# A two-layer encoder on one core: attention masks as extra contraction rows, and high and low tokens in one matmul

## The chip, the cores and the metric

The kernel runs on one core of one Trainium2 chip. The metric is the device time of one execution in microseconds (us). The kernel before takes 827.09 us, the median of three runs from 827.08 to 827.15 us.

## What is computed

Two equal layers over 256 tokens of width 1024, float32. One layer, cut to what matters:

```python
u = rms_norm(x, g_mix_pre)
qa, ka, va, cq, ckv, ga, gb = split(u @ w_in)
# A: 16 query heads, 2 key/value heads of 64; query chunk c (64 tokens) reads key chunks c-1 and c; a sink per head
y_a = swa_sink_attention(rope(qa), rope(ka), va, sinks)
# B: 8 heads of 96 (64 + 32 rotary) from low-rank projections; query chunk c reads key chunks 0..c
y_b = mla_attention(qb, kb, vb)
mixed = sigmoid(ga + b0) * (y_a @ w_oa) + sigmoid(gb + b1) * (y_b @ w_ob)
x = x + rms_norm(mixed @ w_out, g_mix_post)
h = square(relu(rms_norm(x, g_mlp_pre) @ w_mlp_in)) @ w_mlp_out        # 1024 -> 4096 -> 1024
x = x + rms_norm(h, g_mlp_post)
```

Scores that a chunk must not see are set to -1e30 before the softmax.

## The kernel before

Every big product is made of three matmuls on rounded operands: high token times high weight, high token times low weight, low token times high weight. ScalarE copies each weight piece that arrives (`raw`) into a rounded high part (`w_hi`, L582), VectorE subtracts it for the low part (`w_lo`, L853). A piece is at most 128 x 1024 numbers; four high and four low pieces form a ring, so ScalarE may write piece p only when TensorE has used piece p-4 (`piece_used`). Loads are issued by SyncE in order of the pieces.

The order on each engine is written out by hand. One layer goes through:

1. Input projections (pieces 0 to 19), low-rank projections (20 to 27). Between them the rotary turns: VectorE turns the queries of token tile 0, GpSimd everything else (`pool_rope`). TensorE transposes the turned keys (`kA`) and queries (`qA`), VectorE copies the transposes out of the PSUM banks `tp0`, `tp1` (`turned_copy`, L901 to L909).
2. Attention: 18 groups of heads (`QUANTA`): four of kind A on token tile 0 (four heads x 128 keys each), eight of kind A on tile 1 (two heads x 192 keys), two of kind B on tile 0 (four heads x 128 keys), four of kind B on tile 1 (two heads x 256 keys). Step i of 20 on TensorE is: scores of group i, transposes of the probabilities of group i-2, one weight piece of the gate or output products, values of group i-2, and what `EXTRA` lists (a transpose of some q, k or y). The scores (L1251) are float32 matmuls, each recorded as two, with 64 rows of contraction in kind A and 96 in kind B. Behind the heads of a group stands one matmul (L1252) that adds the mask: `chunk_of` (which chunk a query is in) times `mask` (-1e30 or 0 for each key), 256 columns for both kinds of A and B on tile 0, 128 for B on tile 1. Both operands are written once by GpSimd at the start.
3. Output products, the first residual and norm.
4. The MLP, in eight blocks of 512 hidden features. In blocks 1 to 7 the input product (`mlp_in`, L1415 to L1417) has the weights as stationary operand and 256 tokens as moving one: for each of 4 pieces, 4 groups of 128 features and 2 rows of tiles it issues high x high, low tokens x high weights, high tokens x low weights, all into the banks `sc0` and `sc1`. Block 0 goes another way (`first_product`). ScalarE takes the ReLU out of the banks (L650), GpSimd squares it (L493), ScalarE and VectorE split it again (L658, L893), and the output product (`mlp_out`) of a block runs one block later. Blocks 2 to 6 are a loop on every engine.

## Time and profile before

| | |
|---|---|
| median of the runs | 827.09 us |
| profiled execution, its own time | 826.92 us |
| its span in the trace | 825.0 us |
| TensorE matmul busy | 803.2 us (97%), 4613 instructions |
| TensorE weight load busy | 696.4 us (84%) |
| VectorE busy | 509.8 us (62%) |
| ScalarE busy | 408.0 us (49%) |
| GpSimd busy | 125.2 us (15%) |
| chain that ended last | TensorE 92%, VectorE 4%, ScalarE 3% |

The chain that ended last is the row of instructions that sets the end, followed back from the last one. Recorded matmuls overlap: each has a length of its own (a 256-column one 283 ns), while the next starts earlier. What one costs is therefore read from start to start.

### The profile page before, as it was taken

The numbers are of one execution on the slowest core, as the hardware profiler recorded it, in microseconds if no ns is written. First come the engines' busy times: TensorE is split into PE (matmuls) and PEld (weight loads), VectorE is DVE, ScalarE is ACT, GpSimd is POOL, SyncE is SP. The second block draws the span as 40 slices with busy tenths as digits, with TensorE's granted clock in tenths as the row PEclk, the third lists the DMA queues.
The fourth block names the chain that finished last, engine by engine and source line by source line (L and its number), as shares of the span: only waits on it lengthen the run. The fifth ranks groups of instructions, "written<-read, shape, count | busy, mean of one in ns | idle before, by whom it ended". The sixth has DMA issues, their size and how long they took to land.

```text
span 825.0 us, 12057 instructions
## 1 busy us (share of the span) xinstructions
PE 803.2 (97%) x4613; PEld 696.4 (84%) x4613; DVE 509.8 (62%) x685; ACT 408.0 (49%) x747; POOL 125.2 (15%) x204
## 2 busy tenths in 40 slices
PE   6999999999999999999989999999999999999997
PEld 5987878888779999999879788788878899999995
DVE  5768766575785555545566877566576844555554
ACT  5757434444474444444466574444346654444452
POOL 2443000001231000000114420000031200000000
PEclk9999999999999999999999999999999999999999
DMA  7647422334636555565327482331436565565521
GB/s 236 234 159 265 166 71 85 102 102 153 203 115 224 180 186 170 196 203 191 97 72 267 160 297 80 102 102 54 151 126 209 176 201 171 189 200 173 186 103 51
DMA packets 68462, 132.21 MB, mean 160 GB/s; under 512 B 2842, under 2 KB 10564, under 8 KB 68164
## 3 DMA queue, kind: packets, MB, share of 16 engines
q1 hardware_dynamic: 68276, 131.12, 47.9%
q8 instruction: 27, 0.44, 0.2%
q10 hardware_dynamic: 144, 0.52, 0.2%
q14 instruction: 15, 0.12, 0.1%
HBM read 130.59 MB, written 1.05 MB: 160 GB/s over the span
## 4 chain that ended last, share of the span: by engine, by line
PE 92%; DVE 4%; ACT 3%; issue 0%; DMA 0%; POOLq 0%; ACTq 0%; POOL 0%; DVEq 0%
PE acc L1167 17%; PE acc L1169 17%; PE acc L1168 17%; PE sc L1417 7%; PE sc L1416 7%; PE sc L1415 7%; PE tp L1144 5%; PE acc L1283 5%; PE sc L1251 4%; PE acc L1201 4%; ACT s_hi L605 2%; DVE w_lo L853 1%; ACT w_hi L582 1%; PE sc L1167 1%; PE sc L1169 1%; PE sc L1168 1%
## 5 line engine op out<-in xcount | busy, mean ns | idle before, releaser
L853 DVE TENSOR_TENSOR w_lo<-raw,w_hi 128x1024 fp32r<-128x1024 f32 (+3 forms) x256 | 312.8, 1237 | 187.9 <-ACT w_hi L582 186.3
L582 ACT CAST w_hi<-raw 128x1024 fp32r<-128x1024 f32 (+3 forms) x256 | 252.3, 995 | 217.8 <-PE acc L1169 146.6
L1167 PE MATMUL acc<-w_hi,s_hi 128*128 128x512 f32 (+3 forms) x680 | 263.0, 387 | 3.7 <-DVE w_lo L853 3.7
L1168 PE MATMUL acc<-w_lo,s_hi 128*128 128x512 f32 (+3 forms) x680 | 257.6, 379 | 0.0
L1169 PE MATMUL acc<-w_hi,s_lo 128*128 128x512 f32 (+3 forms) x680 | 257.6, 379 | 0.0
L1167 PEld LDWEIGHTS acc<-w_hi,s_hi 128*128 128x128 f32 x680 | 127.9, 188 | 27.9 <-DVE w_lo L853 5.6
L1169 PEld LDWEIGHTS acc<-w_hi,s_lo 128*128 128x128 f32 x680 | 127.8, 188 | 24.0
L1168 PEld LDWEIGHTS acc<-w_lo,s_hi 128*128 128x128 f32 x680 | 128.0, 188 | 21.1
L1415 PE MATMUL sc<-s_hi,w_hi 128*128 128x256 f32 x448 | 126.9, 283 | 0.0
L1417 PE MATMUL sc<-s_hi,w_lo 128*128 128x256 f32 x448 | 126.8, 283 | 0.0
L1416 PE MATMUL sc<-s_lo,w_hi 128*128 128x256 f32 x448 | 126.8, 283 | 0.0
L1415 PEld LDWEIGHTS sc<-s_hi,w_hi 128*128 128x128 f32 x448 | 85.9, 192 | 0.8 <-DVE w_lo L853 0.3
L1416 PEld LDWEIGHTS sc<-s_lo,w_hi 128*128 128x128 f32 x448 | 85.9, 192 | 0.5
L1417 PEld LDWEIGHTS sc<-s_hi,w_lo 128*128 128x128 f32 x448 | 85.9, 192 | 0.0
L493 POOL TENSOR_TENSOR tok<-k_b 128x512 f32<-128x512 f32 x32 | 36.5, 1160 | 266.1 <-ACT k_b L650 266.1
L669 ACT ACTIVATE probs<-sc,neg_m 128x128 f32<-128x128 f32 (+2 forms) x96 | 37.7, 403 | 46.5 <-DVE neg_m L945 32.9
L537 POOL TENSOR_TENSOR tok<-gate_a,gate_b 128x512 f32<-128x512 f32 x8 | 14.1, 1783 | 260.6 <-DVE gate_b L993 260.6
L602 ACT ACTIVATE s_hi<-tp 128x512 fp32r<-128x512 f32 x24 | 13.7, 596 | 48.7 <-PE tp L1144 48.7
L942 DVE TENSOR_REDUCE row_max<-sc 128x2 f32<-128x384 f32 (+2 forms) x36 | 22.6, 627 | 13.8 <-PE sc L1252 13.8
L605 ACT ACTIVATE s_hi<-tp,gain 128x128 fp32r<-128x128 f32 x76 | 21.2, 382 | 15.3 <-PE tp L1144 15.3
L650 ACT ACTIVATE k_b<-sc 128x512 f32<-128x512 f32 x28 | 15.2, 595 | 25.4 <-PE sc L1417 25.4
L883 DVE SCALAR_TENSOR_TENSOR s_lo<-tp,gain,s_hi 128x128 fp32r<-128x128 f32 x76 | 20.7, 343 | 8.8 <-ACT s_hi L605 8.6
(143 smaller groups left out, 779.0 us busy)
## 6 DMA issues: line engine op xcount, KB each, us to landing
raw<-in_w_mlp_in SPq DMA_DIRECT2D x32, 1024.0 KB, 5.3
raw<-in_w_mlp_out SPq DMA_DIRECT2D x32, 1024.0 KB, 5.0
raw<-in_w_in SPq DMA_DIRECT2D x24, 1024.0 KB, 5.4
raw<-in_w_oa SPq DMA_DIRECT2D x8, 1024.0 KB, 5.0
raw<-in_w_out SPq DMA_DIRECT2D x8, 1024.0 KB, 5.0
raw<-in_w_ob SPq DMA_DIRECT2D x4, 1024.0 KB, 5.1
raw<-in_w_in SPq DMA_DIRECT2D x4, 768.0 KB, 4.6
raw<-in_w_in SPq DMA_DIRECT2D x4, 576.0 KB, 7.0
```

The lines of the kernel that those rows point to most:

```text
L582: s.copy(split_view(w_hi, p), raw_view(p)).then_inc(hi_ready, 1)
L605: ins = s.activation(dst[:, k, :], src[:, k, :], ACT.Copy, scale=gain[:, col + k:col + k + 1])
L669: ins = s.activation(probs[:, i % 2, a * w + skip:(a + 1) * w], sc[i % 2][:, a * w + skip:(a + 1) * w], ACT.Exp, bias=neg_m[:, c + a:c + a ...
L853: v.tensor_tensor(split_view(w_lo, p), raw_view(p), split_view(w_hi, p).bitcast(F32), ALU.subtract)\
L1144: ins = nc.tensor.transpose(b[0:rows, i * P:(i + 1) * P], src, ident[:, :])
L1167: mm(banks[t][:, 0:N], h[:, kk, tk], wh[:, k, :], start=(start and k == 0), stop=False)
L1168: mm(banks[t][:, 0:N], h[:, kk, tk], wl[:, k, :], start=False, stop=False)
L1169: ins = mm(banks[t][:, 0:N], low[:, kk, tk], wh[:, k, :], start=False, stop=(stop and k == b - a - 1))
L1283: ins = mm(y[:, (h + a) * 64:(h + a + 1) * 64], pt, vv, start=(b == 0), stop=(b == w // P - 1))
L1415: mm(out, wh[:, k, cols], s1_hi[:, kk, :], start=(i == 0 and k == 0 and f % 2 == 0), stop=False)
L1416: mm(out, wh[:, k, cols], s1_lo[:, kk, :], start=False, stop=False)
L1417: ins = mm(out, wl[:, k, cols], s1_hi[:, kk, :], start=False, stop=(i == 3 and k == 1 and f % 2 == 1))
```

## The change

Three things change.

- Masks. The transposed queries and keys get extra rows in the contraction: two for kind A (64 becomes 66), four for kind B (96 becomes 100). In the query's tile row c is 1 for the queries of chunk c, in the key's tile row c is -1e30 for keys that chunk c must not see. The mask matmul, `chunk_of` and `mask` go. GpSimd writes the rows once, in layer 0, behind the first norm (`chunk_rows`, 20 instructions). For this the queries of kind A stand one head in one tile column, all with partitions 0 to 63, and the tile holds one token tile at a time; the keys of its two heads stand beside each other. The copies out of the transposes become four for the keys (was one) and two for each query transpose (was one). The order of `EXTRA` changes.
- Input product of the MLP, blocks 2 to 7. High and low tokens stand in one tile (`s1_both`); one matmul of 512 columns does high x high and low x high, one of 256 columns does high tokens x low weights. The two halves of a bank hold two partial sums, so the product uses four banks (`sc0`, `sc1`, `tp0`, `tp1`).
- VectorE adds the two halves (`sum_h`, four reductions a block) into `k_b`, and ScalarE takes the ReLU there.

```diff
+            consts = Steps(pool, consts_ready)
+            def chunk_rows(view, low, high, inside, outside):
+                rows, heads, n = view.shape
+                head = view[:, 0, :]
+                consts.link(g.memset(head, inside))
+                consts.link(g.affine_select(out=head, in_=head, compare_op=ALU.is_ge, fill=outside,
+                                            base=-CHUNK * low, pattern=[[1, n]], channel_multiplier=-CHUNK))
...
+                consts.link(g.tensor_copy(view[:, 1:, :], head.unsqueeze(1).to_broadcast([rows, heads - 1, n])))
...
+                if l == 0:
+                    pool.wait_ge(rstd_ready, TT)
+                    chunk_rows(qT_a[AD:AK, :, :], 0, 0, 1.0, 0.0)
+                    chunk_rows(kT_a[AD:AK, :, A_AT[0]], -1, 0, 0.0, NEG)
+                    chunk_rows(kT_a[AD:AK, :, A_AT[1]], 0, 1, 0.0, NEG)
+                    chunk_rows(qT_b[BQK:BK, :, :], 0, 0, 1.0, 0.0)
+                    chunk_rows(kT_b[BQK:BK, :, :], 1 - NCHUNK, 0, 0.0, NEG)
...
+            def relu_of_sum(pos, j):
+                for b in range(2):
+                    act.wait_ge(h_summed, pos.count(TT * (MJ - 2), TT * (j - 2) + b + 1, TT))
+                    s.activation(k_b[:, b, 0:COL], k_b[:, b, 0:COL], ACT.Relu).then_inc(relu_done, 1)
...
+            def sum_h(pos, j, p):
+                dve.wait_ge(piece_used, pos.count(NP, RING + p + 1, 8))
+                for b in range(2):
+                    dve.wait_ge(h_ready, pos.count(TT * MJ, TT * (j - 1) + b + 1, TT))
+                    for f in range(2):
+                        bank = h_banks[2 * b + f]
+                        ins = v.tensor_reduce(k_b[:, b, f * SEQ:(f + 1) * SEQ],
+                                              bank[:, :].rearrange("p (a n) -> p n a", a=2), AX, ALU.add)
+                    ins.then_inc(h_summed, 1)
...
-                    ins = v.tensor_copy(kT_a[:, :], b[:, 0:SEQ])
+                    for g in range(AKV):
+                        for t in range(TT):
+                            ins = v.tensor_copy(kT_a[0:AD, g, A_AT[t]], b[g * AD:(g + 1) * AD, A_KEYS[t]])
...
+                    for odd in range(2):
+                        ins = v.tensor_copy(qT_a[0:AD, g * AG + odd:(g + 1) * AG:2, :],
+                                            b[odd * AD:(odd + 1) * AD, :].rearrange("p (h n) -> p h n", h=AG // 2))
...
-                    mm(b[:, a * w + skip:(a + 1) * w], q, k, start=(a == 0), stop=False)
-                mm(view, chunk_of[r0:r1, :], mk, start=False, stop=True).then_inc(scores_ready, 1)
+                    ins = mm(b[:, a * w + skip:(a + 1) * w], q, k, start=(a == 0), stop=(a == n - 1))
+                ins.then_inc(scores_ready, 1)
...
+                            for k in range(2):
+                                kk = 2 * i + k
+                                mm(bank[:, :].rearrange("p (a n) -> p a n", a=2), wh[:, k, cols], s1_both[:, :, kk, :],
+                                   start=(i == 0 and k == 0), stop=False)
+                                ins = mm(bank[:, SEQ:2 * SEQ], wl[:, k, cols], s1_hi[:, kk, :], start=False,
+                                         stop=(i == 3 and k == 1))
```

TensorE, step 4 of the attention (first group of kind A on tile 1), before. `tp`, `sc` and `acc` are PSUM banks, `probs` the probabilities of the group two steps back:

```order
L1283 MATMUL acc<-kv_a,probsT 128x64 x4
L1144 MATMUL tp<-ident,k_b 96x128 x4
L1251 MATMUL sc<-kT_a,qT_a 128x192 x2
L1252 MATMUL sc<-mask,chunk_of 128x4x64
L1144 MATMUL tp<-ident,probs 128x128 x4
L1167 MATMUL acc<-w_hi,s_hi 128x512
```

The same place on TensorE in the changed kernel:

```order
L1312 MATMUL acc<-kv_a,probsT 128x64 x4
L1181 MATMUL tp<-ident,tok 128x128 x4
L1280 MATMUL sc<-kT_a,qT_a 128x192 x2
L1181 MATMUL tp<-ident,probs 128x128 x4
L1204 MATMUL acc<-w_hi,s_both 128x512
```

The mask matmul is gone, and the transpose ahead of the scores is now one of queries (`tok`), since `EXTRA` is in another order.

VectorE, between the low-rank projections and the first scores, before. The weight pieces behind the copies are those that the last low-rank product and the first gate product need:

```order
L853 TENSOR_TENSOR w_lo<-raw,w_hi 128x512 x2
L901 COPY kT_a<-tp 128x256
L904 COPY qT_a<-tp 128x4x128 x2
L1062 TENSOR_SCALAR neg_sink<-sink_in 128x16
L853 TENSOR_TENSOR w_lo<-raw,w_hi 128x512 x2
L853 TENSOR_TENSOR w_lo<-raw,w_hi 128x1024 x3
```

The same place on VectorE in the changed kernel:

```order
L873 TENSOR_TENSOR w_lo<-raw,w_hi 128x512 x2
L933 COPY kT_a<-tp 64x128
L933 COPY kT_a<-tp 64x192
L933 COPY kT_a<-tp 64x128
L933 COPY kT_a<-tp 64x192
L937 COPY qT_a<-tp 64x4x128 x4
L1095 TENSOR_SCALAR neg_sink<-sink_in 128x16
L873 TENSOR_TENSOR w_lo<-raw,w_hi 128x512 x2
```

Three copies have become eight, in front of the same weight pieces.

VectorE in the MLP loop, from the split of a finished block to the weight pieces of the output product, changed kernel:

```order
L913 TENSOR_TENSOR s_lo<-tok,s_hi 128x512
L872 REGISTER_ALU
L873 TENSOR_TENSOR w_lo<-raw,w_hi 128x1024
L872 REGISTER_ALU
L873 TENSOR_TENSOR w_lo<-raw,w_hi 128x1024
L917 REGISTER_ALU
L919 REGISTER_ALU
L922 TENSOR_REDUCE k_b<-sc 128x256 x2
L919 REGISTER_ALU
L922 TENSOR_REDUCE k_b<-tp 128x256 x2
L873 TENSOR_TENSOR w_lo<-raw,w_hi 128x1024
```

In the kernel before, the two reductions and their register instructions aren't there; the weight pieces follow each other.

## Rows read from the trace of the kernel before

**Rows 1.** Windows: length; busy us (count) of PE, PEld, DVE, ACT, POOL; clock.
```profile
73.00:160.00 87.00, 87.00 (x496) 71.38 (x496) 56.59 (x104) 41.36 (x118) 0.15 (x1) 1.00 0.36 117
262.00:400.00 138.00, 138.00 (x882) 126.02 (x881) 71.75 (x63) 65.30 (x76) 12.25 (x12) 1.00 0.57 186
```
**Rows 2.** Waits of TensorE: total us, times, longest.
```profile
PE acc L1167 <- DVE w_lo L853: 3.7, 4, 1.4
```
**Rows 3.** Timeline of TensorE in the MLP: start, length, instruction.
```profile
299.77 0.28 PE L1415 MATMUL sc<-s_hi,w_hi 128*128 128x256 f32 x1
...
301.09 0.28 PE L1417 MATMUL sc<-s_hi,w_lo 128*128 128x256 f32 x1
...
301.91 0.40 PE L1167 MATMUL acc<-w_hi,s_hi 128*128 128x512 f32 x1
...
311.89 0.39 PE L1169 MATMUL acc<-w_hi,s_lo 128*128 128x512 f32 x1
```
**Rows 4.** Groups by form, TensorE: busy us, mean ns.
```profile
L1415 PE MATMUL sc<-s_hi,w_hi 128*128 128x256 f32 x448 | 126.9, 283 | 0.0
```
**Rows 5.** Timeline of TensorE, step 2 of the attention (kind A).
```profile
80.93 0.60 PE L1144 MATMUL tp<-ident,tok 128*128 128x128 f32 x4
81.46 1.16 PE L1251 MATMUL sc<-kT_a,qT_a 64*128 64x128 f32 x8
82.37 0.36 PE L1252 MATMUL sc<-mask,chunk_of 64*128 64x256 f32 x1
82.67 0.66 PE L1144 MATMUL tp<-ident,probs 128*128 128x128 f32 x4
83.08 0.48 PE L1167 MATMUL acc<-w_hi,s_hi 128*128 128x512 f32 x1
```
**Rows 6.** Timeline of TensorE, step 13 of the attention (kind B).
```profile
147.56 0.61 PE L1144 MATMUL tp<-ident,tok 128*128 128x128 f32 x4
148.00 1.06 PE L1251 MATMUL sc<-kT_b,qT_b 96*128 96x128 f32 x8
148.81 0.36 PE L1252 MATMUL sc<-mask,chunk_of 128*128 128x256 f32 x1
149.02 0.60 PE L1144 MATMUL tp<-ident,probs 128*128 128x128 f32 x4
149.37 0.48 PE L1167 MATMUL acc<-w_hi,s_hi 128*128 128x512 f32 x1
```
**Rows 7.** Timeline of VectorE ahead of the first scores.
```profile
66.19 0.42 DVE L901 COPY kT_a<-tp 128x256 f32<-128x256 f32 x1 [0.43 <-PE tp L1144]
66.62 1.43 DVE L904 COPY qT_a<-tp 128x512 f32<-128x512 f32 x2
...
68.22 0.68 DVE L853 TENSOR_TENSOR w_lo<-raw,w_hi 128x512 fp32r<-128x512 f32 x1
```
**Rows 8.** Timeline of TensorE: first matmul of weight piece 26.
```profile
69.92 0.39 PE L1167 MATMUL acc<-w_hi,s_hi 128*128 128x512 f32 x1
```
**Rows 9.** Groups by form, VectorE.
```profile
L917 DVE COPY probsT<-tp 64x256 f32<-64x256 f32 x16 | 6.6, 415 | 0.0
L942 DVE TENSOR_REDUCE row_max<-sc 128x2 f32<-128x512 f32 x8 | 5.5, 688 | 9.6 <-PE sc L1252 9.6
```
**Rows 10.** Timeline behind the input product of one MLP block.
```profile
368.67 1.09 ACT L650 ACTIVATE k_b<-sc 128x512 f32<-128x512 f32 x2 [1.83 <-PE sc L1417]
...
370.73 3.00 DVE L853 TENSOR_TENSOR w_lo<-raw,w_hi 128x1024 fp32r<-128x1024 f32 x2 [2.63 <-ACT w_hi L582]
...
376.66 0.39 PE L1167 MATMUL acc<-w_hi,s_hi 128*128 128x512 f32 x1
```
**Rows 11.** GpSimd: its costliest group, and the stretch behind the first norm.
```profile
L493 POOL TENSOR_TENSOR tok<-k_b 128x512 f32<-128x512 f32 x32 | 36.5, 1160 | 266.1 <-ACT k_b L650 266.1
...
22.10:59.40 37.30, 37.30 (x216) 33.29 (x215) 26.11 (x37) 22.16 (x44) 16.00 (x23) 1.00 0.56 193
```
**Rows 12.** Timeline of TensorE at the start of layer 1.
```profile
418.94 1.48 PE L1201 MATMUL acc<-w_hi,s_hi 128*128 128x384 f32 x4
```

More of the change, by code:

```diff
@@ L86 @@
 NQ = len(QUANTA)
+CONST_STEPS = 20
 NSTEP = NQ + 2
@@ L206, in build @@
         ident = sb("ident", [P, P])
-        chunk_of = sb("chunk_of", [P, P], F32R)
-        mask = sb("mask", [P, 3, 2 * P], F32R)
         pos_i = sb("pos_i", [P, TT], I32)
@@ L447, in _ @@
             steps.link(ins)
-            sel, mk = chunk_of[:, :].bitcast(F32), mask[:, :, :].bitcast(F32)
-            steps.link(g.memset(sel, 0.0))
-            steps.link(g.memset(mk, 0.0))
-            for half in range(2):
-                r = 2 * 32 * half
-                steps.link(g.memset(sel[r:r + 1, 0:CHUNK], 1.0))
-                steps.link(g.memset(sel[r + 32:r + 33, CHUNK:P], 1.0))
-                steps.link(g.memset(mk[r:r + 1, 0, CHUNK:P], NEG))
-                steps.link(g.memset(mk[r:r + 1, 1:3, P + CHUNK:2 * P], NEG))
-                g.memset(mk[r + 32:r + 33, 1, CHUNK:P], NEG).then_inc(consts_ready, 1)
-                pool.wait_ge(consts_ready, half + 1)
             pool.wait_ge(sines, 2)
@@ L1234, in scores @@
                     pe.wait_ge(probs_ready, pos.count(NQ, i - 1))
-                r0, r1 = (64 * g, 64 * g + 64) if kind == "A" else (0, P)
-                which = 0 if t == 0 else (1 if kind == "A" else 2)
                 b = sc[i % 2]
-                k0 = w // P - 1 if kind == "B" else 0
-                nk = w // P - k0
-                view = b[:, :].rearrange("p (h k c) -> p h k c", h=n, c=P)[:, :, k0:, CHUNK:P]
-                mk = mask[r0:r1, which, 0:w].rearrange("p (k c) -> p k c", c=P)[:, k0:, CHUNK:P]\
-                    .unsqueeze(1).to_broadcast([r1 - r0, n, nk, CHUNK])
                 for a in range(n):
                     if kind == "A":
-                        q = qT_a[r0:r1, h + a, t * P:(t + 1) * P]
-                        k = kT_a[r0:r1, skip:w]
+                        q = qT_a[:, g * AG + h + a, :]
+                        k = kT_a[:, g, A_AT[t]]
                     else:
@@ L1288, in extra @@
                     _, t, h = name
-                    blocks = [tok[:, t, (4 * h + a) * AKV * AD:(4 * h + a + 1) * AKV * AD] for a in range(4)]
+                    blocks = [tok[:, t, (4 * h + a) * 2 * AD:(4 * h + a + 1) * 2 * AD] for a in range(4)]
                 elif name[0] in ("qB", "kB"):
@@ L1342, in _ @@
                 turned(pos, ("qA", 0, 1))
-                pe.wait_ge(consts_ready, 2)
+                pe.wait_ge(consts_ready, CONST_STEPS)
                 for i in range(NSTEP):
@@ L1418, in mlp_in, with mlp_in_wide @@
                         ins.then_inc(piece_used, 1)
+                def mlp_in_wide(pos, p):
+                    for i in range(4):
+                        pe.wait_ge(lo_ready, pos.count(NP, 2 * RAW + p + i + 1, 8))
+                        wh, wl = (split_view(w, p + i).rearrange("p (k n) -> p k n", k=2) for w in (w_hi, w_lo))
+                        for f in range(4):
+                            bank, cols = h_banks[f], slice(f * P, (f + 1) * P)
+                            for k in range(2):
[4 more added lines that the diff above has]
+                                         stop=(i == 3 and k == 1))
+                        ins.then_inc(piece_used, 1)
                 def h_is_split(pos, j):
```

45 lines of the change are left out of this document (28 added, 17 removed), and 4 rows, old and new, of the table EXTRA.

## The prediction, made before the changed kernel ran

> **What bounds the kernel now.** I read the page's busy shares first, then the windows by stage, then the waits of TensorE, and last its timeline from start to start. TensorE is busy in 87.00 of 87.00 us of the attention and in 138.00 of 138.00 us of the MLP, at full clock [rows 1]; VectorE, the next, is busy in 56.59 and 71.75 us of them. The only wait of TensorE on VectorE anywhere is 3.7 us in four pieces [rows 2], and none lies in those two stretches. So the reader should see a kernel whose length is the sum of TensorE's starts: a matmul less is time less, and work on another engine is free until its slack is used up. The question for each part is then what a removed or merged matmul costs from start to start, and whether the added work on VectorE, ScalarE or GpSimd comes late anywhere. The sums are made against the profiled execution, 826.92 us, which is 0.17 us below the median of the runs.
>
> **Input product of the MLP.** In a steady stretch twelve 256-column matmuls stand between 299.77 and 301.09, so 1.32 / 11 = 0.120 us each. Of the 512-column ones 45 stand between 301.91 and 311.89, so 9.98 / 44 = 0.2268 us each [rows 3]. Twice 0.120 is 0.240: one matmul of 512 columns is 0.0132 us cheaper than two of 256. The columns stay, one fixed part per matmul goes. L1415 runs 448 times, which is two layers by seven blocks by 32 [rows 4]; six of the seven blocks change, so 384 pairs are merged: 384 x 0.0132 = 5.1 us, all on TensorE's row of starts. The bounds: nothing, if the moving operand in two stretches or the two half banks cost what the merge saves; and 5.1 us. I take 5.1, since the 512-column row is the same operation with the same number of output columns.
>
> The Trainium skill speaks against this size: "TensorE: Matmul & The Clock Gate", section "Back-to-back issue gap", gives N / 2.4 + 2.5 ns for a warm matmul, which is 109 and 216 ns. By it a merge saves 2.5 ns, the 384 of them 1.0 us, and the total below would be 816.5 us. The trace shows 120 and 226.8 ns, a fixed part of 13 ns; the measurement decides.
>
> What it adds. VectorE does four reductions a block. The nearest row reduces 128x512 in 0.688 us [rows 9], so 2.75 us a block. Behind the input product ScalarE starts its ReLU at 368.67, VectorE ends the low part of the next weight piece half way through its pair of 3.00 us, at 370.73 + 1.50 = 372.23, and TensorE starts on that piece at 376.66 [rows 10]: 4.4 us of slack. In the changed kernel the piece waits in ScalarE's queue behind the ReLU, and the ReLU behind the sums: 368.67 + 2.75 + 0.55 (half of 1.09, the last ReLU) + 1.05 (the copy of a 1024-wide piece) + 1.50 = 374.5. That leaves 2.1 us. So the sums cost nothing: the cover is the first three pieces of the output product. Squares and second split shift by the same 2.3 us, and their user comes a block later.
>
> **Masks.** I compare a step of kind A with one of kind B, in which all else has the same sizes [rows 5, 6]. Kind A has 64 rows in the contraction, kind B 96. From the first transpose ahead of the scores to the first matmul of the product behind them it is 83.08 - 80.93 = 2.15 us in A and 149.37 - 147.56 = 1.81 us in B. The 0.34 us lie at the crossings: 0.09 more before the first score, 0.10 more within the eight records of the scores, 0.09 more behind the mask, 0.06 more in the transposes after it. With 66 rows I expect A to run as B does with 96, since the next row in size above 64 shows no such cost. The mask itself: in B the eight records and the mask take 149.02 - 148.00 = 1.02 us, and eight records at the pace of the transposes (0.44 / 4 = 0.11) take 0.88, so 0.14; a 256-column matmul in a steady row costs 0.12 [rows 3]. I take 0.12, and half of it for the 128-column masks.
>
> Per layer: 12 groups of kind A by (0.34 + 0.12) = 5.5 us, two of B on tile 0 by 0.12 = 0.24, four on tile 1 by 0.06 = 0.24; together 6.0, and 12.0 us for two layers. Bounds: 3.9 us (crossings stay, masks go) and 12.7 (0.14 for each mask). More rows in a float32 matmul add nothing that a row shows: 64 and 96 rows have the same columns and the same pace between.
>
> Here the skill bears the crossings out. "TensorEngine Tiling (Array Packing)", section "Key Properties", says that a change of tiling mode, and not of tile alone, drains TensorE, and its list of modes has 64 rows and 128 rows. By that rule 66 rows leave no change of mode and the saving is the 12.0 us; without it, with masks gone alone, it would be 3.9 us. The difference of the two steps above agrees with the rule.
>
> **Copies that get longer.** The key transposes are copied by four instructions of 64 partitions instead of one. A 64x256 copy takes 0.415 us [rows 9] and a 128x512 one 1.43 / 2 = 0.72 us, so a column costs 0.0012 us and the fixed part is about 0.11. Two of 128 and two of 192 columns: 1.2 us against 0.42 [rows 7], 0.8 more (bounds 0.4 and 1.24, four times the 64x256 row). The second query transpose on TensorE needs the bank that this copy frees, so 0.8 us come straight onto TensorE. The two query copies become four of the same length, as partitions don't shorten a copy (415 ns for 64): 1.43 us more. So VectorE reaches weight piece 26 at 68.22 + 2.2 = 70.4 and ends it at 71.1 us, while TensorE, itself 0.8 later, wants it at 69.92 + 0.8 = 70.7 [rows 7, 8]. Another 0.4 us of wait. Together 1.2 per layer, 2.4 us for two (bounds 0.8 and 4). Before, this wait did not exist, piece 26 was ready 1.0 us early; it is the one new wait that I expect. The next pieces and the row maxima start later by the same 2.2 us, but the steps of the attention give VectorE 30 us of idle time in 87 [rows 1]. The two later query copies (0.72 us more each, in steps 2 and 4) lie in it too.
>
> **GpSimd.** The 20 instructions on the rows handle 960 columns three times and copy 5824: 8704 columns. GpSimd's multiply of 512 takes 1.16 us [rows 11], 2.3 ns per column, so some 20 us; for two or four partitions I know no row, and bound it by 5 and 30. Between the first norm and the second query turn GpSimd is busy 16.00 of 37.30 us [rows 11], so 21.3 are idle. Behind the rows wait the two latent norms, the turn of the keys, the shared rotary key and one query turn; their first user on TensorE is the transpose of the keys at the end of this stretch. I take nothing, 0 to 1 us with what VectorE's own instructions lose beside it. TensorE's wait for `consts_ready` comes later still. The mask rows that GpSimd wrote at the start end nothing that was waited for.
>
> **The sum.** 826.92 - 5.1 - 12.0 + 2.4 = 812.2 us; on the median 812.4.
>
> **Rivals.**
> - A, the merge gives nothing: a two-stretch operand or two partial sums per bank slow the 512-column matmul by 13 ns. For it: no row has such an operand. Against: the mask's own operand was strided and kept its pace. Time: 812.4 + 5.1 = 817.5 us.
> - B, the change does not do what it says for the crossings: 66 rows cross as 64 do. Against: 96 rows don't. Time: 2 x 12 x 0.34 = 8.2 less saved, 820.6 us.
> - C, slower than before: the sums on VectorE. They read a bank with a stride of 256 columns, for which I have no row. If one takes r instead of 0.69 us, the weight piece behind is late once 4 (r - 0.69) exceeds 2.1, at r = 1.2. To lose all of the gain and 0.2% more, 16.4 us over 12 blocks, 1.4 us a block, r must be 1.56. At that point the time is 828.8 us or more. Against: the row maxima run at one column per 1.3 ns, and a stride inside a partition has to cost more than that again.
> - The clock: at the start of layer 1 matmuls of 384 columns start about 1.3 / 4 = 0.32 us apart (each ends 0.2 behind the next start, so 1.48 less 0.2 for four) [rows 12], where 384 columns at the pace of rows 3 take 0.12 + 128 x 0.00042 = 0.17: the clock is at its lower level, 1.2 GHz, behind the pause between the layers. In the changed kernel this stretch may fall away (1.6 us less, from some eleven such matmuls at 0.15) or come at another place. That is no case of its own, it widens the range.
>
> **How the numbers follow.** My forecast has 0.79; its own range is 809.5 to 815.5 (clock 1.6, copies from 0.8 to 4, GpSimd 1). A has 0.10, B 0.07, C 0.04. The range of 8 in 10 takes in A: 809.2 to 817.9. A measurement of this kernel tells a change from none at about 0.2%, 1.7 us: faster by more 0.94 (forecast, A and B, less 0.02), within 0.02 (A and B together with the worst of the copies), slower 0.04 (C).
>
> **What would show it.** Right: L1252 gone; in kind A the transposes, scores and transposes again as close as in kind B, 0.11 us apart; L1459 followed by its partner after 0.227 us and the pair 0.347 us long; TensorE busy all through the MLP; a wait of TensorE of 0.3 to 0.5 us on a `w_lo` ahead of the first scores and a gap of 0.8 in the query transposes, in both layers. Wrong: a wait on `w_lo` or `relu_done` in the MLP (C), a first score 0.1 us late (B), a 512-column matmul in 0.240 us (A), or GpSimd's rows reaching past 59 us with TensorE waiting on the keys.

## The result, and the profile after

The changed kernel takes 816.42 us (median of 4 runs, 815.82 to 818.57), the kernel before beside it 827.12 us: ratio 0.9881, 95% interval 0.9869 to 0.9894. That is 10.7 us faster. The forecast was 812.4 us, its range 809.2 to 817.9. The time lies in the range, 4.0 us above the forecast, and outside the 809.5 to 815.5 that the forecast had for itself. The profiled execution of the changed kernel took 818.57 us (span 816.6), the slowest of its four; part of the reason is the clock, shown below.

I compare the two profiled executions at the ends of the same weight pieces on TensorE. Each number is how much later (+) or earlier (-) the changed kernel is, in us from the start of the span. The ends of the first product in layer 0 differ mostly by the start of the run: TensorE's 384-column matmuls go from 0.32 us apart to 0.17 at 15.5 us before and at 16.0 us after.

| up to | layer 0 | layer 1 | change within the stage |
|---|---|---|---|
| first product, start of the layer | +0.40 | -3.54 | layer 1: +0.78 against the end of layer 0 (clock) |
| last low-rank product ahead of the key transposes | +0.84 | -3.19 | +0.44, +0.35 |
| last matmul ahead of the first scores | +1.94 | -2.09 | +1.10, +1.10 |
| end of the scores and values | -3.23 | -7.26 | -5.17, -5.17 |
| start of the first changed MLP block | -3.2 | -7.2 | 0 |
| last MLP block | -4.32 | -8.34 | -1.09, -1.1 |

So the attention gained 5.2 us a layer where 6.0 were forecast for the masks, the merge gave 2.2 us instead of 5.1, and between the low-rank products and the first scores 2.2 us were lost in the two layers.

Windows of the profile after: one inside the attention, one inside the MLP, one with GpSimd's rows, one around the start of layer 1. Columns as in [rows 1].

```profile
75.00:157.00 82.00, 81.68 (x479) 69.23 (x478) 57.51 (x106) 41.18 (x118) 0.00 (x0) 1.00 0.38 126
259.00:393.00 134.00, 134.00 (x677) 113.36 (x676) 80.29 (x84) 64.16 (x75) 12.51 (x12) 1.00 0.55 186
22.40:39.40 17.00, 17.00 (x123) 16.25 (x122) 14.59 (x21) 12.45 (x29) 15.14 (x22) 1.00 0.81 271
410.00:424.00 14.00, 11.50 (x49) 10.48 (x50) 9.42 (x23) 8.76 (x23) 1.16 (x4) 0.76 0.27 76
```

In the MLP TensorE is still busy in 134.00 of 134.00 us: the sums on VectorE (80 us busy instead of 72 in a like stretch) cost it no wait. In the attention 0.3 us are idle, where [rows 1] had none.

The waits of TensorE after, total us, times, longest (the answer to [rows 2]):

```profile
PE acc L1204 <- DVE w_lo L873: 4.0, 4, 1.6
PE tp L1181 <- DVE kT_a L933: 1.6, 2, 0.8
PE acc L1312 <- DVE probsT L953: 0.4, 2, 0.2
```

The second row is the bank wait of the forecast, 0.8 in each layer. The third was not forecast.

TensorE in the input product of a changed block (the answer to [rows 3]); start, length, instruction:

```profile
332.18 0.40 PE L1459 MATMUL tp<-s_both,w_hi 128*128 128x512 f32 x1
332.42 0.28 PE L1461 MATMUL tp<-s_both,w_lo 128*128 128x256 f32 x1
332.53 0.40 PE L1459 MATMUL tp<-s_both,w_hi 128*128 128x512 f32 x1
332.77 0.28 PE L1461 MATMUL tp<-s_both,w_lo 128*128 128x256 f32 x1
332.89 0.40 PE L1459 MATMUL tp<-s_both,w_hi 128*128 128x512 f32 x1
```

From one wide matmul to the next it is 0.35 to 0.36 us. Over all 384 pairs the mean from start to start is 236.0 ns for the wide one and 116.8 ns for the narrow one, 352.8 for both. The forecast was 347, three separate ones took 360.

TensorE in step 2 of the attention (the answer to [rows 5]):

```profile
82.23 0.60 PE L1181 MATMUL tp<-ident,tok 128*128 128x128 f32 x4
82.66 1.06 PE L1280 MATMUL sc<-kT_a,qT_a 66*128 66x128 f32 x8
83.56 0.60 PE L1181 MATMUL tp<-ident,probs 128*128 128x128 f32 x4
83.91 0.48 PE L1204 MATMUL acc<-w_hi,s_both 128*128 128x512 f32 x1
```

From the first transpose to the product it is 1.68 us, where [rows 5] have 2.15 and the step of kind B in [rows 6] 1.81. The scores' length, 1.06 us for eight, is that of kind B. The first group of the attention is an exception. ScalarE and TensorE there:

```profile
75.15 0.47 ACT L752 ACTIVATE v_b<-acc,rstd 128x256 f32<-128x256 f32 x1
```

```profile
74.58 1.05 PE L1280 MATMUL sc<-kT_a,qT_a 66*128 66x128 f32 x8
75.76 0.47 PE L1204 MATMUL acc<-w_hi,s_both 128*128 128x512 f32 x1
```

From the scores to the product it is 1.18 us here and 0.82 in the second group. The product waits for ScalarE to have copied the last low-rank product out of its bank (`projected(pos, "ukv1")`); that copy ends at 75.62. Before, the mask stood in the same time (1.20 us), so of the 0.46 us that a group gains elsewhere the first one gains only 0.1, in both layers. The forecast had no term for it.

VectorE ahead of the first scores (the answer to [rows 7]), and in step 4:

```profile
67.02 1.13 DVE L933 COPY kT_a<-tp 64x128 f32<-64x128 f32 x4 [0.42 <-PE tp L1181]
68.18 2.81 DVE L937 COPY qT_a<-tp 64x512 f32<-64x512 f32 x4
...
70.99 2.42 DVE L873 TENSOR_TENSOR w_lo<-raw,w_hi 128x512 fp32r<-128x512 f32 x3
...
94.42 1.38 DVE L937 COPY qT_a<-tp 64x512 f32<-64x512 f32 x2
95.83 0.56 DVE L975 TENSOR_REDUCE row_max<-sc 128x2 f32<-128x384 f32 x1
96.42 0.16 DVE L978 SCALAR_TENSOR_TENSOR neg_m<-row_max,neg_sink 128x2 f32<-128x2 f32 x1
96.50 0.69 DVE L953 COPY probsT<-tp 128x512 f32<-128x512 f32 x1
```

The key copies take 1.13 us (1.2 forecast), the four query copies 2.81. In step 4 two copies of queries stand ahead of the maxima and of the copy of the probabilities, which so ends at 97.19. TensorE wants it earlier. Its rows at the bank wait, at the late piece, and in step 4:

```profile
66.82 0.60 PE L1181 MATMUL tp<-ident,tok 128*128 128x128 f32 x4
68.21 0.66 PE L1181 MATMUL tp<-ident,tok 128*128 128x128 f32 x4 [0.78 <-DVE kT_a L933]
...
71.23 0.39 PE L1206 MATMUL acc<-w_hi,s_lo 128*128 128x512 f32 x1
71.72 0.50 PE L1204 MATMUL acc<-w_hi,s_hi 128*128 128x512 f32 x1
72.06 0.39 PE L1205 MATMUL acc<-w_lo,s_hi 128*128 128x512 f32 x1
...
96.67 0.39 PE L1206 MATMUL acc<-w_hi,s_both 128*128 128x512 f32 x1
97.25 1.10 PE L1312 MATMUL acc<-kv_a,probsT 128*128 128x64 f32 x8 [0.19 <-DVE probsT L953]
```

Between 71.23 and 71.72 there are 0.49 us where 0.23 is the pace, and 0.34 to the next one: the wait on piece 26, 0.4 us with what follows it. Between 96.67 and 97.25 there are 0.58 us where step 3 has 0.23: the new wait of step 4. The values behind it take 0.1 us more too.

The clock. Before has a stretch at 1.2 GHz (granted clock 0.5) of 3.41 us at the start of layer 1. The profiled execution after has one of 6.83 us, twice as long, and so shows 0.76 as the mean of 410 to 424 us. In three of its four runs the mean granted clock was 0.999 or 1.0, in the profiled one 0.995, and that one is 1.9 us slower than the next.

### The profile page after: what moved, and what is told of

It reads as the page before. It is cut to its first block, busy times and chain, and to the rows that moved or that the text cites. A ratio compares the mean times of both kernels' runs of the same rounds, so it can differ in the third digit from the quotient of the medians.

```text
span 816.6 us, 11325 instructions
## 1 busy us (share of the span) xinstructions
PE 791.9 (97%) x4193; PEld 672.9 (82%) x4193; DVE 539.2 (66%) x747; ACT 408.9 (50%) x747; POOL 142.2 (17%) x212
## 4 chain that ended last, share of the span: by engine, by line
PE 87%; DVE 8%; ACT 3%; DMA 1%; issue 1%; SPq 0%; POOLq 0%; POOL 0%; ACTq 0%; DVEq 0%
PE acc L1204 16%; PE acc L1206 16%; PE acc L1205 16%; PE tp L1459 6%; PE sc L1459 6%; PE acc L1312 5%; PE tp L1181 4%; PE acc L1238 4%; PE sc L1280 3%; DVE w_lo L873 3%; PE tp L1461 3%; PE sc L1461 3%; ACT s_both L619 1%; ACT w_hi L596 1%; DVE qT_a L937 1%; PE sc L1445 1%
## 5 line engine op out<-in xcount | busy, mean ns | idle before, releaser
L1204 PE MATMUL acc<-w_hi,s_both 128*128 128x512 f32 (+2 forms) x352 | 135.2, 384 | 1.4 <-DVE w_lo L873 1.0
L1204 PE MATMUL acc<-w_hi,s_hi 128*128 128x512 f32 (+1 forms) x328 | 128.2, 391 | 3.2 <-DVE w_lo L873 3.0
L1206 PE MATMUL acc<-w_hi,s_both 128*128 128x512 f32 (+2 forms) x352 | 131.2, 373 | 0.0
L1205 PE MATMUL acc<-w_lo,s_both 128*128 128x512 f32 (+2 forms) x352 | 131.2, 373 | 0.0
L1206 PE MATMUL acc<-w_hi,s_lo 128*128 128x512 f32 (+1 forms) x328 | 126.7, 386 | 0.0
L1205 PE MATMUL acc<-w_lo,s_hi 128*128 128x512 f32 (+1 forms) x328 | 126.5, 386 | 0.0
L1204 PEld LDWEIGHTS acc<-w_hi,s_both 128*128 128x128 f32 x352 | 66.3, 188 | 13.9 <-DVE w_lo L873 2.6
L1206 PEld LDWEIGHTS acc<-w_hi,s_both 128*128 128x128 f32 x352 | 66.2, 188 | 11.7
L1204 PEld LDWEIGHTS acc<-w_hi,s_hi 128*128 128x128 f32 x328 | 61.6, 188 | 16.4 <-DVE w_lo L873 4.7
L1205 PEld LDWEIGHTS acc<-w_lo,s_both 128*128 128x128 f32 x352 | 66.4, 189 | 10.1
L1205 PEld LDWEIGHTS acc<-w_lo,s_hi 128*128 128x128 f32 x328 | 61.6, 188 | 11.3
L1459 PE MATMUL tp<-s_both,w_hi 128*128 128x512 f32 x192 | 70.0, 398 | 0.0
L1459 PE MATMUL sc<-s_both,w_hi 128*128 128x512 f32 x192 | 69.9, 398 | 0.0
L551 POOL TENSOR_TENSOR tok<-gate_a,gate_b 128x512 f32<-128x512 f32 x8 | 14.1, 1782 | 250.9 <-DVE gate_b L1026 250.9
```

The lines of the kernel that those rows point to most:

```text
L1204: mm(banks[t][:, 0:N], h[:, kk, tk], wh[:, k, :], start=(start and k == 0), stop=False)
L1205: mm(banks[t][:, 0:N], h[:, kk, tk], wl[:, k, :], start=False, stop=False)
L1206: ins = mm(banks[t][:, 0:N], low[:, kk, tk], wh[:, k, :], start=False, stop=(stop and k == b - a - 1))
L1459: mm(bank[:, :].rearrange("p (a n) -> p a n", a=2), wh[:, k, cols], s1_both[:, :, kk, :], start=(i == 0 and k == 0), stop=False)
```

## The experiments

Each kernel is the changed one with one edit, unless said otherwise. The kernel before had 826.97 us beside the first four, 827.0 beside the next four and 826.93 beside the last four. Runs of one kernel lie up to 3.6 us apart, so sums of small terms are read from the traces and the medians confirm them.

**The two halves of the change apart.** First the masks alone: the MLP's input product, its ReLU and VectorE's order as before, so no sums.

```diff
-                    mlp_in_wide(here, 76)
+                    mlp_in(here, 76)
```

> The changed kernel with the MLP of before (three 256-column matmuls, two banks, ReLU out of the banks); masks stay as contraction rows. Theory (each part acts alone on TensorE's row of starts): the trace of the changed kernel shows that TensorE gained 1.12 us per layer in the MLP, so this kernel should be 2.2 us slower than the changed one and some 8.5 us faster than before, near 818.6 us. Rival (the parts meet: the sums on VectorE cost something elsewhere, or the masks' gain depends on the MLP): the two parts alone do not add up to the gain of both within 1 us. By the sizes of the prediction it would be 817.5 us.

Measured: 819.54 us (819.18 to 820.19), ratio 0.9910, 0.9896 to 0.9924. The masks with all their costs are worth 7.4 us.

Then the merge alone: the kernel before with `s1_both`, `mlp_in_wide` and the sums.

> The kernel before with the MLP of the changed one; masks, copies and GpSimd as before. Theory: 384 pairs of 512 and 256 columns take 0.353 us in place of three of 0.120, so 384 x 0.007 = 2.8 us less, less 0.5 us for edges of the blocks: 827.1 - 2.3 = 824.8 us. By the prediction's term (0.0132 us for each merge) it would be 5.1 us less, 822.0 us. Rival A of the prediction (the merge gives nothing): 827.1 us.

Measured: 824.94 us (823.69 to 827.27), ratio 0.9978, 0.9968 to 0.9988. The merge alone is worth 2.0 us, and its wide and narrow matmuls start 236 and 117 ns apart, as in the changed kernel. So the merge fell short by itself, whatever the masks do beside it. Together the halves give 9.4 us, the changed kernel 10.7; the spreads of the runs cover the rest.

**The crossings.** The scores of kind A contract rows 0 to 63 only. The masks of kind A are so left out, what the kernel returns is wrong, and only its time is read.

```diff
-                        q = qT_a[:, g * AG + h + a, :]
-                        k = kT_a[:, g, A_AT[t]]
+                        q = qT_a[0:AD, g * AG + h + a, :]
+                        k = kT_a[0:AD, g, A_AT[t]]
```

> The changed kernel, but the scores of kind A use only rows 0 to 63 of the tiles: the masks of kind A are left out of the computation, and nothing else changes. Theory (the crossing between 64 and 128 rows costs 0.34 us a group, whatever the mask matmul is): TensorE's starts before and behind the scores of the 24 groups of kind A open again, 24 x 0.28 to 24 x 0.34 = 6.7 to 8.2 us slower than the changed kernel, some 823.5 us. Rival (the gain came from the mask matmul that is gone, with its own operands and accumulation, not from the rows): no slower than the changed kernel, 816.4 us, and starts of the transposes behind the scores 0.11 us after the last score.

Measured: 823.91 us (823.17 to 824.92), ratio 0.9961, 0.9948 to 0.9974. Its step 2:

```profile
82.49 0.60 PE L1181 MATMUL tp<-ident,tok 128*128 128x128 f32 x4
83.02 1.16 PE L1280 MATMUL sc<-kT_a,qT_a 64*128 64x128 f32 x8
84.11 0.66 PE L1181 MATMUL tp<-ident,probs 128*128 128x128 f32 x4
84.52 0.48 PE L1204 MATMUL acc<-w_hi,s_both 128*128 128x512 f32 x1
```

Two rows fewer make the kernel 7.5 us slower. The step takes 84.52 - 82.49 = 2.03 us against 1.68 with 66 rows: a crossing costs 0.35 us here, and the mask matmul was the other 0.12 of the 2.15 before. Step 4, a group of two heads on tile 1, with 64 rows and then in the changed kernel:

```profile
93.49 0.61 PE L1181 MATMUL tp<-ident,tok 128*128 128x128 f32 x4
...
95.28 0.48 PE L1204 MATMUL acc<-w_hi,s_both 128*128 128x512 f32 x1
```

```profile
92.59 0.61 PE L1181 MATMUL tp<-ident,tok 128*128 128x128 f32 x4
...
94.05 0.48 PE L1204 MATMUL acc<-w_hi,s_both 128*128 128x512 f32 x1
```

That is 1.79 against 1.46 us, so the crossing costs as much with two heads as with four; all eight groups of tile 1 differ by 0.34 us. On tile 0 the four groups differ by 0.0 (the first, which waits for the bank in the changed kernel), 0.37, 0.34 and 0.29 us. The run with 64 rows has no wait in step 4, 0.34 to its credit. Together that is 3.4 us, and the traces differ by 3.42 and 3.45 us in the attention of the two layers. Rival B is out.

**Why the merge gives less.** Is it the operand in two stretches? The two kinds of token lie side by side for each k:

```diff
-        s1_both = sb("s1_both", [P, 2, KD, SEQ], F32R)
+        s1_both = sb("s1_both", [P, KD, 2, SEQ], F32R)
```

> The changed kernel with high and low tokens of one tile side by side in memory, so that the 512 columns of the merged matmul are one stretch of 2 KB per partition in place of two that lie 8 KB apart. Theory 1 (two stretches cost the 9 ns by which the 512-column matmul of the MLP, 236 ns, is slower than the plain one, 227 ns): it comes down to 227, the kernel is 384 x 0.009 = 3.5 us faster, some 813.0 us. Theory 2 (the 9 ns come from the alternation of 512 and 256 columns, or of the banks' halves): no change, 816.4 us.

Measured: 817.82 us (816.10 to 818.71), ratio 0.9892, 0.9878 to 0.9907; the pair again 236 and 117 ns. The stretches cost nothing. The median is 1.4 us above the changed kernel's, but the profiled run (816.10) is not; the other three had a mean granted clock of 0.994 to 0.996, where three of the changed kernel's four had 0.999 or 1.0.

Is it the alternation of widths? First two wide, then two narrow ones in each bank; then all eight wide ones of a piece and then its eight narrow ones. The edit of the second:

```diff
                                 mm(bank[:, :].rearrange("p (a n) -> p a n", a=2), wh[:, k, cols], s1_both[:, :, kk, :],
                                    start=(i == 0 and k == 0), stop=False)
+                        for f in range(4):
+                            bank, cols = h_banks[f], slice(f * P, (f + 1) * P)
+                            for k in range(2):
+                                kk = 2 * i + k
                                 ins = mm(bank[:, SEQ:2 * SEQ], wl[:, k, cols], s1_hi[:, kk, :], start=False,
                                          stop=(i == 3 and k == 1))
```

> The changed kernel with the order of the merged product changed: per bank first both 512-column matmuls, then both 256-column ones, in place of 512, 256, 512, 256. Theory (each change of width between neighbours costs some ns: the pair takes 353 ns where 120 + 227 = 347 were expected): half of the changes go, the mean pair comes to 350 ns, 384 x 0.003 = 1.2 us faster than the changed kernel. Rival (the merged matmul itself is slower, with four banks or two partial sums): the 512-column one stays at 236 and the 256-column one at 117 ns, no gain.

> The same, but for each weight piece all eight 512-column matmuls first, then all eight 256-column ones. Theory (changes of width cost): only one change in eight is left, the mean pair comes to 348 ns, 384 x 0.0055 = 2.1 us faster than the changed kernel, 814.3 us if that is 816.4. Rival: as for the order by bank, no gain.

Measured: two by two 815.67 us (814.17 to 816.52), ratio 0.9864, 0.9844 to 0.9884; eight by eight 814.60 us (813.60 to 816.53), ratio 0.9861, 0.9838 to 0.9883. The second one's timeline:

```profile
330.87 0.64 PE L1465 MATMUL sc<-s_both,w_lo 128*128 128x256 f32 x4
331.35 0.64 PE L1465 MATMUL tp<-s_both,w_lo 128*128 128x256 f32 x4
331.82 1.09 PE L1459 MATMUL sc<-s_both,w_hi 128*128 128x512 f32 x4
```

Four narrow ones take 331.35 - 330.87 = 0.48 us, so 0.120 each, the old pace. Mean over all pairs: 348.0 ns two by two, 348.3 eight by eight, against 352.8 alternating. Two changes of width within four matmuls cost about the same in total as two within sixteen, so it isn't a fixed price for each change. Over the MLP of the two layers the trace of the eight-by-eight order is 2.1 us ahead of the changed kernel's.

Does it cost to add to columns that the matmul just ahead wrote? In the changed kernel each narrow one does. So does each in the order two by two, where four in a row go to one bank, and that order has 348.0 ns; it answers the question already. In the order eight by eight half of the narrow ones add to columns that were written longer ago. As a second test no narrow matmul adds to what the one just ahead wrote, and the widths still change nearly every time:

```diff
-                        for f in range(4):
-                            bank, cols = h_banks[f], slice(f * P, (f + 1) * P)
-                            for k in range(2):
...
+                        for k in range(2):
+                            kk = 2 * i + k
+                            for f in range(5):
+                                if f < 4:
+                                    mm(h_banks[f][:, :].rearrange("p (a n) -> p a n", a=2), wh[:, k, f * P:(f + 1) * P],
+                                       s1_both[:, :, kk, :], start=(i == 0 and k == 0), stop=False)
+                                if f > 0:
+                                    ins = mm(h_banks[f - 1][:, SEQ:2 * SEQ], wl[:, k, (f - 1) * P:f * P], s1_hi[:, kk, :],
+                                             start=False, stop=(i == 3 and k == 1))
```

> The widths still alternate in the MLP input, but a narrow matmul adds to the bank of the wide one before the last, not to the columns that the matmul just ahead of it wrote. Theory (the change of width costs): the pair stays at 352 to 353 ns, and the time at 816.4. Rival (adding to columns that have just been written costs): the pair falls to 348 or 347 ns, 384 x 5.3 ns = 2.0 us, 814.4, and the grouped orders gained for that reason.

Measured: 816.30 us (814.83 to 816.88), ratio 0.9865, 0.9849 to 0.9880; wide and narrow together 352.8 ns, the same as the changed kernel's to a tenth. Adding to columns just written costs nothing. But the order here is wide, wide, narrow, wide, narrow, wide, narrow, narrow: the width changes six times in eight matmuls, where the changed kernel has eight changes (352.8), the order two by two four (348.0) and the order eight by eight one (348.3). Two changes fewer gained nothing, so it isn't the number of changes. In both orders that gain, two matmuls of one width in a row also go to the same bank; here they go to different ones. Whether that is the condition no run shows. What is shown is that the order decides over 5 ns a pair; why is open.

**Rival C: the room behind the sums.** Every reduction is done a second time, into spare columns.

```diff
+                        spare = k_b[:, b, COL:COL + SEQ] if f == 0 else kv_a[:, b, 0:SEQ]
+                        ins = v.tensor_reduce(spare, bank[:, :].rearrange("p (a n) -> p n a", a=2), AX, ALU.add)
```

> Each of the four reductions a block is done a second time, into spare columns; nothing reads them. It tests the room behind the sums. Prediction's sizes: 2.1 us of room a block, the second four take 4 x 0.688 = 2.75, so 0.65 x 12 = 7.8 us more, 824.2. Theory from the trace after: the low part of the weight piece behind the sums is done at 347.72 and TensorE starts on it at 350.07, 2.35 us of room, so 0.40 x 12 = 4.8 us more, 821.2. Rival: the sums have far more room than that (the pieces catch up from a lead that the trace doesn't show), and the time stays at 816.4; or they are on the path already, and it is 12 x 2.75 = 33 us more, 849.

Measured: 817.92 us (817.33 to 818.69), ratio 0.9888, 0.9873 to 0.9903: 1.5 us more, less than either size. VectorE and TensorE behind the input product, at the place of [rows 10]:

```profile
346.31 0.68 DVE L922 TENSOR_REDUCE k_b<-tp 128x256 f32<-128x512 f32 x1
346.91 0.68 DVE L925 TENSOR_REDUCE kv_a<-tp 128x256 f32<-128x512 f32 x1
349.23 2.44 DVE L873 TENSOR_TENSOR w_lo<-raw,w_hi 128x1024 fp32r<-128x1024 f32 x2 [1.64 <-ACT w_hi L596]
```

```profile
350.42 0.39 PE L1208 MATMUL acc<-w_hi,s_lo 128*128 128x512 f32 x1
350.65 0.44 PE L1206 MATMUL acc<-w_hi,s_hi 128*128 128x512 f32 x1
```

The weight piece is ready at about 349.23 + 1.22 = 350.45, and TensorE starts on it at its usual 0.23 us behind the last matmul: the room is just used up. In the changed kernel the piece is ready at 347.72 and TensorE starts on it at 350.30, so the room was 2.6 us, not 2.1. Both sizes of the expectation were too large for two reasons: reductions in a row start 0.60 us apart, not 0.688 (346.91 less 346.31 for the last two), so four more take 2.4 us; and my room from the trace ended at the last matmul of the piece before, one matmul early. Within the MLP this trace loses 0.3 us a layer to the changed kernel's. Another 0.85 us are lost between the first product and the first scores of layer 0. Of them 0.3 lie ahead of the end of the last low-rank product before the key transposes, where TensorE waits 2.16 us for its weight piece instead of 1.64; the other 0.55 lie behind it, where the clock fell to 1.2 GHz from 66.46 to 69.88, after that wait. The window from 66 to 70 us, whose column before the last two is the granted clock (1.00 in the changed kernel's):

```profile
66.00:70.00 4.00, 3.63 (x16) 2.96 (x15) 3.42 (x9) 1.56 (x3) 2.58 (x4) 0.57 0.97 302
```

No other trace has that. The other three runs of this kernel have a mean granted clock of 0.996 against 0.994 in the profiled one, so they probably lack one such stretch, and how the 1.5 us of the median are made up stays open. Rival C is out by a wide margin: sums twice as long are hardly felt.

**The copies.** The second query transpose goes behind piece 24 on TensorE, and VectorE prepares piece 27 ahead of its copies.

```diff
 # VectorE
                 turned(pos, ("qA", 0, 0))
+                lo(pos, 27)
                 turned(pos, ("qA", 0, 1))
 # TensorE
-                        extra(pos, ("qA", 0, 1))
...
+                        if c == 2 and i == 0:
+                            extra(pos, ("qA", 0, 1))
```

> The changed kernel with the second query transpose of tile 0 moved on TensorE behind the first weight piece of the product that follows, and on VectorE its copies moved behind the low parts of weight pieces 26 and 27. Theory (the longer copies cost TensorE 0.7 us in the wait for the bank and 0.4 for piece 26 in each layer, since they stand in front of both): both waits go, what is left is at most the 0.4 us for piece 28: 2.2 us faster than the changed kernel, 814.2 us. Rival (VectorE is full there, so a wait only moves to piece 27 or 28 or to the scores): less than 0.8 us faster.

Measured: 815.14 us (814.17 to 815.74), ratio 0.9862, 0.9845 to 0.9880. Between the key transposes and the first scores its trace gains 1.4 us on the changed kernel's in each layer, and the wait on `kT_a` is gone from its waits:

```profile
PE acc L1205 <- DVE w_lo L873: 4.0, 4, 1.6
...
PE acc L1313 <- DVE probsT L953: 0.4, 2, 0.2
```

1.4 is more than the 1.1 lost by the change: before, the second transpose also waited 0.24 us for its bank. The median shows 1.3 of these 2.8 us; the rest is within the spread.

**GpSimd's rows first.** The mask rows are built at the start, ahead of the tables, as the kernel before did with its masks.

> The changed kernel with GpSimd's 20 instructions on the mask rows put at its start, ahead of the rotary tables, in place of behind the first norm. Theory (in layer 0 they only slow VectorE's low parts beside them, 0.25 us at piece 11 and 0.3 us at piece 23): TensorE 0.5 us earlier ahead of the attention in layer 0, some 815.9 us. Rival 1 (they cost nothing): same time as the changed kernel. Rival 2 (the tables and the first norm come late): slower by some us.

Measured: 818.37 us (817.06 to 819.18), ratio 0.9899, 0.9880 to 0.9918. The median is 2.0 us above the changed kernel's, though the runs of the two overlap (815.82 to 818.57). In the trace the 0.4 us lost beside GpSimd's rows are won back, and the first product ends 1.5 us later. About half of these 1.5 us is the clock of this run: TensorE's 384-column matmuls go from 0.32 us apart to 0.17 at 17.6 us, in the changed kernel at 16.0 us, and in two other runs with the same start at 14.1 and 17.1 us. The other half is four late weight pieces of 0.16 us each. VectorE's weight pieces of the first 18 us, in the changed kernel and with the rows first:

```profile
L873 DVE TENSOR_TENSOR w_lo<-raw,w_hi 128x768 fp32r<-128x768 f32 x4 | 3.7, 955 | 3.5 <-ACT w_hi L596 3.5
```

```profile
L871 DVE TENSOR_TENSOR w_lo<-raw,w_hi 128x768 fp32r<-128x768 f32 x4 | 5.1, 1312 | 3.0 <-ACT w_hi L594 3.0
```

The same four instructions take 1312 ns on average instead of 955. The first two run beside GpSimd's rows and take 3.28 us together instead of 1.92; the last two run when the rows are done and take 1.81, as in the changed kernel. Where the change has put the rows, later pieces grow in the same way, with less on the path.

**Both gains together, and one step more.** The eight-by-eight order with the later copies:

> The two edits that gave something, together: all wide matmuls of a piece ahead of its narrow ones, and the second query transpose with its copies behind piece 24. Theory: they act in different stages and add. The pair of the MLP input falls from 353.3 to 348.3 ns, 384 x 5.0 ns = 1.9 us; the waits of the bank and of pieces 26 and 28 go, 1.4 us a layer in the trace of the run with the later copies, 2.8 us. Sum 816.4 - 4.7 = 811.7. Rival: each run so far lay within the spread that the clock windows give (about 2 us between runs of one kernel), and the two gains are in part that; then the time is 814 or more.

Measured: 811.64 us (811.25 to 812.02, 5 runs), ratio 0.9813, 0.9800 to 0.9827. The two add up, and the time is 4.8 us below the changed kernel. Then the fourth query transpose moves on by a step:

```diff
-EXTRA = {1: [("qA", 1, 0)], 3: [("qA", 1, 1)],
-         4: [("qB", 0, 0)], ...
+EXTRA = {1: [("qA", 1, 0)], 3: [("qB", 0, 0)],
+         4: [("qA", 1, 1)], ...
```

> As the kernel with both edits, and the fourth query transpose of kind A trades its step with the first one of kind B: its two copies (1.38 us) then stand ahead of the copy of the probabilities in step 5, where VectorE normalises nothing, and the single copy of kind B (0.69 us) stands in step 4. Theory: the wait of the values on the probabilities in step 4 (0.577 instead of 0.16 us ahead of the first value matmul) goes, 0.4 us a layer, 0.8 in all: 0.8 below the kernel with both edits, 810.9. Rival: step 5 has no more room than step 4, the wait only moves by a step, and the time stays at that of both edits, 811.7; or TensorE now waits in step 3 for GpSimd's last rotation, which the fourth step hid.

Measured: 811.04 us (810.31 to 812.52, 5 runs), ratio 0.9814, 0.9799 to 0.9828. Its waits of TensorE:

```profile
PE acc L1205 <- DVE w_lo L873: 4.0, 4, 1.6
PE acc L1239 <- DVE w_lo L873: 0.5, 2, 0.3
```

The wait on `probsT` is gone, and step 4 is 0.45 us shorter in each layer against the kernel with both edits. The median moves by 0.6, which the two spreads don't tell apart. These two are the best kernels of the study, both faster than the kernel before and than the changed one.

## Why the prediction was right, and where it was off

- **What bounds the kernel: right.** TensorE's row of starts sets the time, and every gain or loss was found in it. VectorE took 29 us more work and cost 3 us, all at three places with a wait. [rows 2] are not the only wait on VectorE, as the prediction has it: two more, 0.5 us together, stand in the first product (L1201, on L853), at a place that the change doesn't touch.
- **The merge: the mechanism right, the size wrong.** The step that failed is "The columns stay, one fixed part per matmul goes", with 384 x 0.0132 = 5.1 us. It priced both matmuls from stretches in which all had one width. Measured were 7.2 ns a merge, 2.8 us by the gaps and 2.2 us by the ends of the pieces. With equal widths together it is 11.7 ns, 4.5 us, close to the forecast. The forecast's own sign for it, a pair of 0.347 us, showed it at once: it was 0.353. Rival A named the 512-column matmul at 0.240 us, and it came to 0.236, yet its narrow partner got 3 ns back, and A's two reasons don't hold: with the tokens in one stretch the pair stays at 353, and with two sums in each bank it comes to 348 once the order is changed.
- **The 816.5 us that followed from the rule of the Trainium skill** ("TensorE: Matmul & The Clock Gate", section "Back-to-back issue gap") lies beside the median of 816.42 by luck: a merge saves 7.2 ns alternating and 11.7 grouped, not 2.5. The page gives the formula for an isolated matmul, and this is a stream of them.
- **The masks: right.** Forecast 12.0 us for both layers. The attention gained 5.17 us in each with the 0.4 us wait of step 4 inside it, so the masks gave about 5.6, 11.2 in all. The crossing at 0.34 us was right for four heads and for two. The missing 0.4 a layer is the first group, whose gain ends at a bank that ScalarE hasn't emptied yet; the prediction had counted all 12 groups alike. That 66 rows cross as little as 96 was right. Its bounds are off by 0.1: 12.0 less 8.2 is 3.8, not 3.9, and 0.14 for each mask gives 12.6.
- **The copies: the forecast waits right, one missed.** Bank wait 0.70 us (0.8 forecast), piece 26 0.40 (0.4 forecast), 1.1 in place of 1.2 a layer. "The two later query copies (0.72 us more each, in steps 2 and 4) lie in it too" failed for the second: step 4 also normalises, and the 30 us of idle time in the attention don't lie in that step. It cost 0.4 us a layer. Together 3.0 us, not 2.4.
- **The sums: right.** They cost nothing. The room was 2.6 us, not 2.1.
- **GpSimd: nearly right.** The rows took 22.50 to 39.25, 16.8 us (20 forecast). Nothing waited for them; what they cost, some 0.5 us in layer 0, is VectorE's and GpSimd's own instructions growing longer beside each other, which the 0 to 1 us allowed for. Another 0.25 to 0.35 us are lost in the input and low-rank projections of layer 1, where no rows are written; in the changed kernel they lie at a late weight piece, between 457.58 and 458.07. All eleven traces with the rows behind the norm have it; the one with the rows first and the one with the merge alone have none (0.0). A multiplication that VectorE does ahead of that piece takes 1.58 us there instead of 1.26 in the kernel before. Why it does is open.
- **The sum of it.** By the profiled executions: 812.2 + 2.9 (merge) + 0.8 (masks, nearly all of it the first group) + 0.6 (copies) + 0.5 (GpSimd) = 817.0. The profiled run took 818.57: 0.4 more at the start, 0.8 at the lower clock and 0.35 on a piece at the start of layer 1 make 818.55. The median, with the clock low for less, is at 816.42. It lies inside the range because the range had room for rival A; the 809.5 to 815.5 of the forecast alone were missed, by the merge above all.

## What to carry to other kernels

Read the price of a matmul as the distance of two starts, and in the order in which it will run: a price from a row of equal ones isn't that of a mixed row, and merging calls paid nearly in full here only when like widths stood together, in twos or eights. When copies or sums go to an engine with time to spare, look for the room at the very step where they stand, since the busy share of the stage hides the one step that is full. A few contraction rows more can be cheaper than none, where they spare the crossing between products of 64 rows and of 128.

## What the runs showed of the hardware

- Matmuls of 512 and 256 columns in turn start 236 and 117 ns apart, 353 for both. With two of a kind in a row, both on one bank, or with eight in a row, two on each of four banks, it is 348, and a stretch of only one kind has 227 or 120. In the order wide, wide, narrow, wide, narrow, wide, narrow, narrow, with neighbours on different banks, it stays at 353. Whether the operand lies in one stretch or two changes nothing.
- A score matmul of 66 or 100 rows between ones of 128 costs no crossing; one group of 64 rows costs 0.34 to 0.35 us, whether it has four heads or two. "TensorEngine Tiling (Array Packing)" in the Trainium skill, section "Key Properties", says that a change of mode drains TensorE. The run with 64 rows agrees: 0.34 us a group.
- VectorE's subtraction of 768 columns takes 955 ns while GpSimd is idle and 1640 ns (3.28 us for two) beside GpSimd's writes to two or four partitions. GpSimd's instructions grow as well: the copy of 1792 columns below takes 2.56 us, and an equal one 5 us earlier took 1.68. On two or four partitions GpSimd isn't cheap (mean ns of one last):

```profile
L498 POOL COPY qT_a<-qT_a 2x1920 f32<-2x1920 f32 x1 | 2.2, 2192 | 0.1
L498 POOL COPY kT_b<-kT_b 4x1792 f32<-4x1792 f32 x1 | 2.6, 2557 | 0.1
```

- A reduction over two halves of a bank, with a stride of 256 columns, takes as long as one over neighbours (681 to 686 ns against 688 in [rows 9]):

```profile
L922 DVE TENSOR_REDUCE k_b<-sc 128x256 f32<-128x512 f32 x24 | 15.5, 686 | 6.9 <-PE tp L1461 6.9
```

- The stretch at 1.2 GHz at the start of layer 1 varies from run to run. Profiled executions of this family had none, 3.41 us or 6.83 us of it, and the four runs of the changed kernel have mean granted clocks from 0.995 to 1.0. From the end of layer 0 to the end of layer 1's first product it is 15.6 us with none (the kernel with the tokens side by side), 15.6 to 16.4 us in the ten traces with 3.41 us, and 16.8 to 17.0 us in the three with 6.83 us. So the long stretch costs 1.3 to 1.4 us, and a short one can cost nothing, where it falls among TensorE's waits.
